# Centring the retention values in the weights instead of in the transposing matmul, and y turned before the conv roots are spread

## The reference

```python
proj = rmsnorm(x, mix_norm_w) @ w_in
q, k = rotary(proj_q), rotary(proj_k) * 128 ** -0.5
v = proj_v.reshape(b, s, 4, 128)
y = retention(q, k, v, forward) + retention(q, k, v, backward)   # sums over tokens of weight * v
mu = mean(y, axis=-1)                                            # over the 128 columns of a head
y = (y - mu) * rsqrt(mean((y - mu) ** 2) + EPS)
y = silu(proj_g) * (y * gn_w + gn_b)
# the other group: depthwise conv of 31 taps over tokens, layernorm, silu
```

## Time and profile before

| What | Value |
|---|---|
| median of 3 runs | 2952.61 us (2951.25 to 2954.43) |
| profiled execution | 2954.14 us, of which the span from the first to the last instruction is 2952.2 us |
| TensorE matmul busy | 2821.5 us, 96% of the span |
| VectorE, ScalarE, GpSimd busy | 1366.0, 549.1 and 888.6 us |
| granted TensorE clock, mean | 0.98 of full |
| a column of the projection | 156.1 us |
| retention with the conv's norm | about 700 to 935 us of the span |

### The profile page before, as it was taken

How to read it: one execution, slowest core, us unless ns; L and a number is a source line. 1 busy time by engine, 2 the same in 40 slices (tenths; PEclk the granted TensorE clock), 3 DMA queues, 4 the chain that set the end, 5 groups by cost and what they waited for, 6 DMA issues and landing times.

```text
span 2952.2 us, 37368 instructions
## 1 busy us (share of the span) xinstructions
PE 2821.5 (96%) x14050; PEld 2388.8 (81%) x14050; DVE 1366.0 (46%) x1534; ACT 549.1 (19%) x950; POOL 888.6 (30%) x443
## 2 busy tenths in 40 slices
PE   5899999996898999999999999989999999999998
PEld 4788888885887898888888888778988888888887
DVE  4593939496765433532514224443335324142343
ACT  5211111112354322100100001232221000010012
POOL 1242524333872100233323333310003233333331
PEclk8999999998889999999999999999999999999999
DMA  4133333336644222111111113232231111111111
GB/s 158 50 111 125 104 114 118 120 114 224 211 144 156 93 86 86 50 50 50 43 49 50 45 48 107 64 107 88 83 95 43 50 50 43 50 50 49 44 50 71
DMA packets 289755, 254.01 MB, mean 86 GB/s; under 512 B 8016, under 2 KB 253960, under 8 KB 283400
## 3 DMA queue, kind: packets, MB, share of 16 engines
q1 hardware_dynamic: 266320, 203.45, 22.3%
q10 hardware_dynamic: 23352, 49.39, 4.5%
HBM read 196.71 MB, written 56.10 MB: 86 GB/s over the span
## 4 chain that ended last, share of the span: by engine, by line
PE 77%; DVE 14%; DMA 3%; issue 2%; ACT 2%; POOL 1%; DVEq 0%; ACTq 0%; SPq 0%; POOLq 0%
PE ps L681 22%; PE ps L676 21%; PE ps L677 21%; DVE acc L1651 10%; PE ps L1036 2%; PE ps L1038 2%; PE ps L1037 2%; PE ps L900 1%; PE ps L828 1%; DMA wqk_d<-pst 1%; PE ps L998 1%; DVE alo L1938 1%; DMA out<-rows 1%; PE ps L1047 0%; DMA wb<-wqk_d 0%
## 5 line engine op out<-in xcount | busy, mean ns | idle before, releaser
L537 POOL TENSOR_SCALAR whi<-wraw 128x1024 fp32r<-128x1024 f32 x192 | 231.0, 1203 | 1903.9 <-PE ps L681 1186.5
L676 PE MATMUL ps<-ahi,whi 128*128 128x512 f32 x1376 | 542.3, 394 | 17.4 <-DVE alo L1938 11.6
L677 PE MATMUL ps<-alo,whi 128*128 128x512 f32 x1376 | 537.8, 391 | 0.0
L539 POOL TENSOR_TENSOR wlo<-wraw,whi 128x1024 fp32r<-128x1024 f32 x192 | 529.8, 2760 | 16.0
L676 PE MATMUL ps<-bhi,whi 128*128 128x512 f32 x1024 | 399.4, 390 | 2.3 <-DVE blo L1859 2.3
L677 PE MATMUL ps<-blo,whi 128*128 128x512 f32 x1024 | 398.4, 389 | 0.0
L1651 DVE SCALAR_TENSOR_TENSOR acc<-upad,taps,acc 128x2048 f32<-128x2048 f32 x120 | 346.6, 2888 | 15.7 <-DVE acc L1648 0.6
L681 PE MATMUL ps<-ahi,wlo 128*128 128x512 f32 x1376 | 340.2, 389 | 0.0
L676 PE MATMUL ps<-xhi,whi 128*128 128x512 f32 x768 | 305.5, 398 | 18.7 <-DVE xlo L1582 11.2
L676 PEld LDWEIGHTS ps<-ahi,whi 128*128 128x128 f32 x1376 | 259.5, 189 | 78.3 <-DVE alo L1938 14.9
L677 PE MATMUL ps<-xlo,whi 128*128 128x512 f32 x768 | 303.7, 395 | 0.0
(11 more groups left out here) (264 smaller groups left out, 3637.1 us busy)
## 6 DMA issues: line engine op xcount, KB each, us to landing
wraw<-in_w_ff SPq DMA_DIRECT2D x128, 512.0 KB, 3.9
proj_d<-st ACTq DMA_DIRECT2D x64, 256.0 KB, 2.5
wraw<-in_w_in SPq DMA_DIRECT2D x24, 512.0 KB, 4.7
xt<-in_x SPq DMA_DIRECT2D x16, 512.0 KB, 6.7
wraw<-in_w_xkv SPq DMA_DIRECT2D x16, 512.0 KB, 5.6
vwo_d<-pst ACTq DMA_DIRECT2D x16, 512.0 KB, 3.7
wqk_d<-pst ACTq DMA_DIRECT2D x16, 512.0 KB, 4.1
wraw<-in_w_out SPq DMA_DIRECT2D x16, 512.0 KB, 5.1
```

Of the source, the lines that this page charges most:

```text
L537: pool.tensor_scalar(whi[:, slot, :, :], wraw[:, slot, :, :], 1.0, 0.0, ALU.mult, ALU.add).then_inc(w_hi, 1)
L539: pool.tensor_tensor(wlo[:, slot, :, :], wraw[:, slot, :, :], whi[:, slot, :, :], ALU.subtract).then_inc(w_ready, 1)
L676: nc.tensor.matmul(o, whi[:, slot, k, :], hi(k), start=(k == order[0]), stop=False)
L677: nc.tensor.matmul(o, whi[:, slot, k, :], lo(k), start=False, stop=False)
```

## The change

The weight block of v is centred over its 128 columns in place in `wraw` by VectorE, once per column of the projection, between tap 12 and tap 13 (`CEN = 13`). Two instructions do it: a sum over each run of 128 into `v_mean`, and a multiply and add of the broadcast mean. GpSimd waits for this (`v_cen`) before it splits the block. In retention, the values are turned by plain transposes with `ident`. `cen_mat`, the GpSimd instruction that made it and the wait for it are gone. `turn_back(h)` stands ahead of `conv_spread(h)`.

```diff
-        alloc(es, "to_4096", [P, 16], F32)
+        v_mean = alloc(es, "v_mean", [P, KT], F32)
+        alloc(es, "to_4096", [P, 8], F32)
...
-            cen_mat = b2("cen_mat", (P, P))
...
+        CEN = 13
...
                 proj_split(c, "O1", done(c, "q3"))
+                wait_alone(pool, v_cen, c + 1)
                 proj_split(c, "v", 1 + 2 * c + 2, o_mm)
...
-            pool.tensor_tensor(cen_mat[:, :], ident[:, :], mean_mat[:, :], ALU.subtract).then_inc(iot, 1)
...
                 pe.wait_ge(l_v, 16 * h + 16)
-                pe.wait_ge(iot, 1)
...
-                        last = pe.matmul(ps[:, token_bank(h, j, 0), c * P:(c + 1) * P], vb[:, cc * P:(cc + 1) * P], cen_mat[:, :],
-                                         start=True, stop=True)
+                        last = pe.transpose(ps[:, token_bank(h, j, 0), c * P:(c + 1) * P], vb[:, cc * P:(cc + 1) * P], ident[:, :])
...
                     value_tokens(h + 1)
+                    turn_back(h)
                     conv_spread(h)
-                    turn_back(h)
...
-                taps_of(0, 16)
+                def centre_values():
+
+                    dve.wait_ge(w_full[0], 16 * FILLS * c + 16 * NTH["v"] + 16)
+                    dve.tensor_reduce(v_mean[:, :], wraw[:, 0, :, :], AX.X, ALU.add).then_inc(v_sum, 1)
+                    dve.wait_ge(v_sum, c + 1)
+                    dve.scalar_tensor_tensor(out=wraw[:, 0, :, :], in0=v_mean[:, :].unsqueeze(2).to_broadcast([P, KT, P]), scalar=-1.0 / P,
+                                             in1=wraw[:, 0, :, :], op0=ALU.mult, op1=ALU.add).then_inc(v_cen, 1)
+
+                taps_of(0, CEN)
+                centre_values()
+                taps_of(CEN, 16)
```

More of the change, by code:

```diff
@@ L271, in build @@
         kt_mm, vt_mm, kt_ev, vt_ev = sem("kt_mm"), sem("vt_mm"), sem("kt_ev"), sem("vt_ev")
-        v2 = sem("v2")
+        v2, v_sum, v_cen = sem("v2"), sem("v_sum"), sem("v_cen")
         kvf_mm, kvb_mm, f_scan, b_scan = sem("kvf_mm"), sem("kvb_mm"), sem("f_scan"), sem("b_scan")
@@ L1311, in _ @@
             leave_phase(act)
-            act.wait_ge(iot, 6)
+            act.wait_ge(iot, 5)
             for h in range(HEADS):
@@ L1701, in decay_masks @@
             def decay_masks():
-                dve.wait_ge(iot, 6)
+                dve.wait_ge(iot, 5)
                 dve.tensor_scalar(io_t[:, 1, :], io_t[:, 0, :], 0.0, None, ALU.max).then_inc(dpos, 1)
```

## The result

The changed kernel takes 2963.0 us (median of 7 runs), the kernel before 2954.4 us on the same chip; the ratio is 1.0033, with an interval of 1.0023 to 1.0042. So it is slower, by about 9.7 us after that ratio (0.33% of 2952.6; the two medians lie 8.6 us apart), where +6.8 us was forecast. The profiled execution has a span of 2958.6 us against 2952.2.

The account below looks back on a forecast made before the run. VectorE was taken to bound each projection column from a3 to M1, TensorE the rest; in retention, scan and TensorE's queue end together. Centring +9.7 and retention -2.9 gave +6.8 us, 2959.4 us, range 2955 to 2965.

Parts of the forecast that it names:

- The split of v: Projection, GpSimd: starts 3.4 us later, high part ready about 169.5 us, ends about 174.3, still in time for TensorE.
- v1's store: Projection, ScalarE: comes at about 188.8 us, so v2 waits about 1 us for its bank, hidden.
- the term of +9.7 us for the centring: Projection, between a3 and M1: two unhidden VectorE instructions cost 2.4 us in each of four columns.
- the fourth rival: Projection: late VectorE costs more than its own time, by a clock fall or another tap meeting; about 2963 us, 17%.
- the 1.9 us of a tap's meeting: Projection: a VectorE tap running beside GpSimd's split of v takes longer, one such meeting being worth 1.9 us.
- the sum: Whole kernel: centring +9.7 and retention -2.9 give +6.8 us, 2959.4 us.
- Its other form: Projection: GpSimd's split meets one more VectorE tap, costing 1.9 us a column, reckoned for two of four columns.
- -2.9: Retention: 0.7 us gained at each of two changes of head plus 1.5 us in head 3's tail.
- the spread's end: Retention: behind the turned y the spread ends at s + 6.3, formerly s + 6.4, s being the start of `value_tokens`.
- the first rival: Retention: the gain gets through whole, 1.95 us a change of head instead of 0.7; 2955.6 us, 27%.
- The centring is hidden: Projection: VectorE has 2.4 us or more to spare before M1, only -2.9 remains; 2949.7 us, 5%.
- the transposes do raise the clock: Retention: the forecast assumed this; the rival that they don't makes `scores_in` 3.7 us later three times, about 2973 us, 6%.

Follow-up runs that it names:

- experiment 6: Kernel before with only the centring's reduction added, its sum unused, GpSimd waiting for it; 2957.9 us, 1.0018.
- experiment 3: Changed kernel with `conv_spread` put back ahead of `turn_back`; 2959.6 us, 1.0020 against the kernel before.
- experiment 7: Changed kernel with `low(K1)` and `query_low(1)` ahead of the last two taps and the convolution's store behind the next column's first loads; 2951.4 us, 0.9997.
- experiment 1: Kernel before with only the centring of the weights added, retention left as it was; 2969.6 us, 1.0051.
- experiment 4: Changed kernel with `low(K1)` and `query_low(1)` ahead of the last two taps; 2961.6 us, 1.0037 against the kernel before.
- experiment 5: Kernel before with `low(K1)` and `query_low(1)` ahead of the last two taps; 2960.6 us, 1.0031.
- experiment 8: Kernel before with `query_low(1)` ahead of the last two taps and the convolution's store behind the next column's first loads; 2953.2 us, 1.0001.

## Why the prediction was right, and by how much it was off

**Right: where the cost lies.** M1 waits for VectorE in all four columns, and what VectorE has to do more there lengthens the column. Its two instructions take 1.21 and 1.23 us (forecast 1.21 and 1.22), and the taps did not become dearer on balance. The reduction alone cost 1.07 us a column (experiment 6). The split of v was done earlier than forecast, its high part at 167.4 us and its low part at 171.8 instead of 169.5 and 174.3: with a start 3.4 us later, the prediction's own rows give 173.0. V2 waited 0.82 us for v1's store, for about 1 forecast.

**Missed: the term of +9.7 us for the centring**, which measured 14.6. Four times 2.45 us are VectorE's own time, and the column whose clock held has exactly that, a period of 158.55 us for 158.5 forecast. The rest is the clock that fell behind three of the four pauses: 4.63, 4.46 and 4.63 us of M1 instead of 3.13 to 3.14, 4.3 us in all. Of the 0.5 us left over, half lies in the first column, where VectorE idles 0.50 us before a tap instead of 0.27. That is the fourth rival, which had 17% and 2963 us; that it named the very time is luck, since it reckoned with two columns at the 1.9 us of a tap's meeting, not with three falls at 1.3 to 1.5. It should have been in the sum: the prediction itself put TensorE's pause at 1.9 to 2.5 us (it was 2.48 to 2.77), and priced the fall only in a rival. Its other form, a split that meets one more tap, did not come.

**Retention: right in mechanism, -3.4 us for -2.9.** The norm took over as bound and the heads gained 2.3 us up to `scores_in` of head 3 (12.2 us late at `q_rot` of head 1, 9.9 at `scores_in`), for 2.1. `value_tokens` took 3.54, 3.87 and 3.87 us for 3.6, and `chunk_states` came 2.1, 1.8 and 1.3 us closer to its start for 1.95. In head 3 GpSimd's splits hold up the gating, as foreseen:

```profile
880.94 2.37 POOL L540 TENSOR_TENSOR wlo<-wraw,whi 128x1024 fp32r<-128x1024 f32 x1
883.28 4.97 POOL L606 TENSOR_TENSOR y_b<-y_b,g_in 128x512 f32<-128x512 f32 x4
```

What the prediction did not ask is whether the moved line was the cause. It compared the spread's end with that of before (s + 6.3 against s + 6.4; its rows give s + 6.5) and not with what it would be if the spread had stayed where it was. In experiment 3 the norm, which follows the spread, starts 4.6, 5.2 and 4.5 us behind the start of `value_tokens`. In the changed kernel it starts at 6.2, 7.7 and 7.3 us, the last two this late because `turn_back` ran in part at the lower clock. The move costs some 3 us, and without it the gain of the transposes comes through whole, as the first rival had it.

**The rivals that fell.** The gain got through whole only in the old order. The centring is hidden only where M1 no longer waits for it (experiment 7). And the transposes do raise the clock. In the changed kernel TensorE ran nothing but transposes from 832.65 to 839.33 us:

```profile
836.00:837.00 1.00, 1.00 (x7) 1.00 (x6) 1.00 (x1) 0.74 (x2) 1.00 (x1) 0.50 0.00 0
837.00:838.00 1.00, 1.00 (x6) 1.00 (x5) 1.00 (x1) 0.97 (x2) 1.00 (x2) 0.50 0.29 49
838.00:839.00 1.00, 1.00 (x8) 1.00 (x7) 0.26 (x1) 1.00 (x1) 1.00 (x1) 0.56 0.85 287
839.00:840.00 1.00, 1.00 (x7) 0.71 (x6) 0.00 (x0) 1.00 (x3) 1.00 (x1) 1.00 1.02 434
```

The clock rises before 839 us, ahead of the spread's first product. Here the trace does not agree with the Trainium skill (TensorE: Matmul & The Clock Gate, Part 4: PE-mode transpose), by which a run of transposes leaves the full clock disengaged. It rose late, though: `turn_back` took 3.17 us where it takes 1.91 at the upper level.

**The account.** 14.6 - 3.4 = +11.2 us up to the store of y; 8.8 of it is seen there, since this execution's first column began 2.4 us early. The runs say 9.7 us, with an interval of 6.8 to 12.4. The profiled spans differ by 6.4 us: the other 2.4 us go between the store and the end, where nothing is changed and the profiled executions differ by up to 8 us. Part of the closeness of the forecast is luck, then: the centring's term was 4.9 us too small, and the time came out only 2.9 us above the sum.

## What to carry over

When work is added to the engine that another one waits for, its price is not only its length: write down how long the waiting TensorE will stand still, and look at the granted clock behind pauses of that length. A few thrown-away products can be cheaper than the fall. Where an order is changed together with a faster step, cost each of the four combinations; here the faster step was worth 0.23% and the new order took 0.10% back. And before a wait is taken from one queue, look for the next thing released by the same instruction: moving `query_low(1)` early won nothing in the changed kernel and cost the one before 0.3%, until the store in SyncE's queue was moved as well.

## What the hardware showed that was not expected

- The clock fell behind 9 of 12 pauses of 2.47 to 2.77 us before M1 (the changed kernel, experiments 1 and 3), behind none of the four of 2.13 us (experiment 6). The length alone doesn't decide: in experiment 4 it held behind a pause of 2.94 us and fell behind two of 2.53 and 2.52 us; in experiment 5 it fell behind 2.46 and 2.38 us and held behind 2.06. What separates them stays open.
- In all kernels with the full centring VectorE idles before one tap per column, 0.50 us in the first and 0.26 to 0.27 in the others. With the reduction alone it does not. The cause is open.
- `diag`, 128 x 512 on VectorE, took 4.92 us at one change of head in the changed kernel, 4.91 in the one before and at most 1.92 in experiment 3, with GpSimd at work in all. The long ones began just behind the start of a GpSimd instruction of 4.5 us and ended 0.5 to 0.6 us behind its end (in the changed kernel 833.34 to 838.26 us, beside 833.18 to 837.70); the one of 1.02 us in experiment 3 began 0.5 us before such an instruction ended. In the changed kernel TensorE was busy until after its end, so it cost nothing; where the old order meets the long one, as in experiments 5 and 8, the spread waits for it (0.07 and 0.25 us).
